# RMS norm sums in four 32-column strips behind the first early panel, with the gain folded into the operand split

## What is computed

```python
def rmsnorm(x, w):
    xf = x.astype(jnp.float32)
    y = xf * lax.rsqrt(jnp.mean(xf * xf, axis=-1, keepdims=True) + EPS)
    return (y * w.astype(jnp.float32)).astype(x.dtype)

def swiglu(h, w_gate, w_up, w_down):
    return (jax.nn.silu(h @ w_gate) * (h @ w_up)) @ w_down
...
    for layer in range(DEPTH):
        x = x + 0.5 * swiglu(rmsnorm(x, norm_ffn1[layer]), ffn1_gate[layer], ffn1_up[layer],
                             ffn1_down[layer])
        x = x + hybrid_mixer(rmsnorm(x, norm_mix[layer]), lb_all[layer], w_in[layer], hg_norm_w[layer],
...
        x = x + 0.5 * swiglu(rmsnorm(x, norm_ffn2[layer]), ffn2_gate[layer], ffn2_up[layer],
                             ffn2_down[layer])
    return rmsnorm(x, norm_final)
```

## Time and profile before

| | before |
|---|---|
| median of 3 runs | 1942.34 us |
| the profiled execution, its own time | 1941.35 us |
| its span in the trace | 1939.5 us |
| PE busy | 1803.8 us (93%) |
| PEld busy | 1736.4 us (90%) |
| DVE busy | 1086.5 us (56%) |
| ACT busy | 917.3 us (47%) |
| granted TensorE clock, mean | 0.971 |

### The profile page before, as it was taken

How to read it: one execution, slowest core, us unless ns; L and a number is a source line. 1 busy time by engine, 2 the same in 40 slices (tenths; PEclk the granted TensorE clock), 3 DMA queues, 4 the chain that set the end, 5 groups by cost and what they waited for, 6 DMA issues and landing times.

```text
span 1939.5 us, 34227 instructions
## 1 busy us (share of the span) xinstructions
PE 1803.8 (93%) x15120; PEld 1736.4 (90%) x15120; DVE 1086.5 (56%) x1231; ACT 917.3 (47%) x966; POOL 169.6 (9%) x120
## 2 busy tenths in 40 slices
PE   7999998899999999989889999999999888889997
PEld 7999897789999999988779999879897778889986
DVE  5544688464446544678555444644455555555555
ACT  5433675454335333566445344544444454534444
POOL 0000061000000000052000000683000000000000
PEclk9999998899999999998889999999999999999998
DMA  7555442135555555453035555456255414445541
GB/s 250 168 185 178 150 140 88 45 109 181 189 175 169 178 181 189 143 153 119 22 99 174 175 186 184 150 176 206 87 174 164 161 45 152 136 152 177 193 154 42
DMA packets 206531, 291.00 MB, mean 150 GB/s; under 512 B 4560, under 2 KB 170576, under 8 KB 206128
## 3 DMA queue, kind: packets, MB, share of 16 engines
q1 hardware_dynamic: 205936, 287.04, 45.4%
q0 software_dynamic: 448, 1.77, 0.3%
HBM read 287.75 MB, written 1.05 MB: 149 GB/s over the span
## 4 chain that ended last, share of the span: by engine, by line
PE 81%; DVE 11%; ACT 5%; issue 2%; DMA 0%; SPq 0%; ACTq 0%; DVEq 0%
PE colb L788 52%; PE acc L788 27%; DVE w_lo L1511 3%; PE aux L788 2%; ACT w_hi L1161 2%; DVE arena L1716 1%; DVE u L1571 1%; DVE x L1614 1%; DVE op_lo L1577 0%; DMA raw<-ffn_gate 0%; PE colb L1097 0%; ACT arena L1474 0%; DVE u L1629 0%; DVE x L1620 0%; DVE arena L1774 0%
## 5 line engine op out<-in xcount | busy, mean ns | idle before, releaser
L1511 DVE TENSOR_TENSOR w_lo<-raw,w_hi 128x2048 fp32r<-128x2048 f32 x271 | 622.1, 2296 | 625.6 <-ACT w_hi L1161 625.4
L1161 ACT ACTIVATE w_hi<-raw 128x2048 fp32r<-128x2048 f32 x271 | 515.7, 1904 | 430.5 <-PE acc L788 246.8
L788 PE MATMUL colb<-u_hi,w_hi 128*128 128x256 f32 x2256 | 644.2, 286 | 16.0 <-DVE w_lo L1511 15.9
L788 PE MATMUL colb<-u_lo,w_hi 128*128 128x256 f32 x2256 | 641.7, 284 | 0.0
L788 PE MATMUL colb<-u_hi,w_lo 128*128 128x256 f32 x2256 | 641.7, 284 | 0.0
L788 PEld LDWEIGHTS colb<-u_hi,w_hi 128*128 128x128 f32 x2256 | 436.5, 193 | 18.0 <-issue 11.9
L788 PEld LDWEIGHTS colb<-u_lo,w_hi 128*128 128x128 f32 x2256 | 436.7, 194 | 0.1
L788 PEld LDWEIGHTS colb<-u_hi,w_lo 128*128 128x128 f32 x2256 | 436.5, 193 | 0.0
L788 PE MATMUL acc<-op_hi,w_hi 128*128 128x256 f32 x1328 | 381.7, 287 | 22.5 <-DVE op_lo L1566 14.3
L788 PE MATMUL acc<-op_lo,w_hi 128*128 128x256 f32 x1328 | 379.5, 286 | 0.0
L788 PE MATMUL acc<-op_hi,w_lo 128*128 128x256 f32 x1328 | 379.1, 285 | 0.0
(11 more groups left out here) (298 smaller groups left out, 1784.1 us busy)
## 6 DMA issues: line engine op xcount, KB each, us to landing
raw<-w_in SPq DMA_DIRECT2D x78, 1024.0 KB, 5.1
raw<-ffn_gate SPq DMA_DIRECT2D x44, 1024.0 KB, 5.3
raw<-ffn_up SPq DMA_DIRECT2D x44, 1024.0 KB, 5.4
raw<-ffn_down SPq DMA_DIRECT2D x44, 1024.0 KB, 4.9
raw<-w_up SPq DMA_DIRECT2D x16, 1024.0 KB, 5.5
raw<-w_down SPq DMA_DIRECT2D x16, 1024.0 KB, 4.9
raw<-w_out SPq DMA_DIRECT2D x8, 1024.0 KB, 4.9
raw<-w_ret_out SPq DMA_DIRECT2D x8, 1024.0 KB, 4.9
```

The lines of the kernel that those rows point to most:

```text
L788: return pe.matmul(o, a, b, start=start, stop=stop, skip_group_check=True)
L1161: act.activation(split_view(w_hi, r), raw[:, p % RAW_SLOTS, 0:r["kt"] * r["nc"]], ACT.Copy)\
L1511: tt(split_view(w_lo, r), raw[:, p % RAW_SLOTS, 0:r["kt"] * r["nc"]], split_view(w_hi, r).bitcast(F32), ALU.subtract).then_inc(sem("w_lo_r ...
```

## The change

What it does, for each of the nine norms that feed a stage:

- On PE the norm sum no longer stands ahead of panel p. PE goes through panel p by chunks (`kk` outside, both halves `m` inside), and so through every column panel of kinds "A" and "B". Behind panel p come eight float32 matmuls with 32 columns of ones each, two for each of four strips of 32 output partitions (`parts`). ACT copies these partial sums to `rstd`, and in the middle of panel p+1 (`kk == 4`) one float32 matmul of the full ones matrix adds them (`parts_sum`, into the other half of `aux`). Since the strips hold 32 equal rows each, the scale of Ln is 1/(32 D).
- On ACT the rounding of `x * gain` reads `x` with the gain as the scale of the activation, two instructions of 128x256 for a chunk, with no wait for DVE. `w_hi` of p+1 stands between chunk 1 and chunk 2 instead of behind all; the squares of chunks 2 and 3 come last.
- On DVE `x_gained` is gone; the low part is one `scalar_tensor_tensor` of `x`, the gain and `op_hi` (two of 128x256 for a chunk), and `fill` makes `u32` from `x`, gain and `rstd` in the same way. `w_lo` of panel p is taken out of the panel before and stands behind the first chunk's update.

```diff
@@ -329,17 +329,17 @@
             early[1] = dict(n=count["fill"], panel=len(panels), ops=len(ops), **more)
             return count["fill"]
 
-        def norm_sum(src, next_="x_update"):
+        def norm_sum(src, next_="x_update", **more):
             count["norm"] += 1
-            step("norm_sum", n=count["norm"], src=src, x=count["x"], group=count["group"], next=next_, fill=count["fill"])
+            step("norm_sum", n=count["norm"], src=src, x=count["x"], group=count["group"], next=next_, fill=count["fill"], **more)
             return count["norm"]
 
         def pre_norm(gain, at):
 
 
             step("gained", gain=gain, at=at, n=count["fill"] + 1)
-            n = norm_sum("x", "fill")
-            f = fill(norm=n)
+            n = norm_sum("x", "fill", gain=gain, at=at)
+            f = fill(norm=n, gain=gain, at=at)
             return f
 
         def x_update(kind, **more):
@@ -828,26 +828,47 @@
                         if r["half"] == 1 and m == 0:
                             last.then_inc(sem("wide_first"), 1)
                 else:
-                    for m in range(max(r["nc"] // P, 1)):
-                        o = colb[:, r["c"] % 3, T * m:T * m + T]
-                        for kk in range(r["kt"]):
-                            xh, xl = r["xop"](kk)
-                            if m == 0 and kk % 2 == 0 and r.get("gained"):
-                                pe.wait_ge(sem("gained"), 4 * (r["gained"] - 1) + kk // 2 + 1)
-                            if m == 0 and kk % 2 == 0 and u_ready:
-                                pe.wait_ge(sem("u_ready"), u_ready - 3 + kk // 2)
+                    for kk in range(r["kt"]):
+                        xh, xl = r["xop"](kk)
+                        if kk % 2 == 0 and r.get("gained"):
+                            pe.wait_ge(sem("gained"), 4 * (r["gained"] - 1) + kk // 2 + 1)
+                        if kk % 2 == 0 and u_ready:
+                            pe.wait_ge(sem("u_ready"), u_ready - 3 + kk // 2)
+                        if kk == 4 and r.get("half") == 1:
+                            parts_sum(r)
+                        for m in range(max(r["nc"] // P, 1)):
+                            o = colb[:, r["c"] % 3, T * m:T * m + T]
                             m_ = slice(P * m, P * m + P)
...
                             for i, (a, b) in enumerate(trio):
-                                last = mm(o, a, b, kk == 0 and i == 0, kk == r["kt"] - 1 and i == 2)
+                                last = mm(o, a, b, kk == 0 and m == 0 and i == 0, kk == r["kt"] - 1 and i == 2)
+                    if r.get("gained"):
+                        last.then_inc(sem("panel_used"), 1)
+                        parts(r["norm"])
+                        return
                 last.then_inc(sem("panel_used"), 1)
 
+            def parts(n):
+
+                if n == 1:
+                    pe.wait_ge(sem("ones_set"), 1)
+                pe.wait_ge(sem("sq_ready"), 4 * n)
+                for kk in range(KD):
+                    g = slice(32 * (kk % 4), 32 * (kk % 4) + 32)
+                    last = mm(aux[g, 0:T], ones[:, 0:32], sq[:, kk, :], kk < 4, kk >= 4)
+                last.then_inc(sem("norm_parts"), 1)
+
+            def parts_sum(r):
+
+                pe.wait_ge(sem("parts_copied"), r["fill"]["n"])
+                mm(aux[:, T:2 * T], ones, rstd[:, :]).then_inc(sem("norm_summed"), 1)
+
             def norm_sum(r):
-                if r["n"] == 1:
-                    pe.wait_ge(sem("ones_set"), 1)
+                if r["next"] == "fill":
+                    return
                 for kk in range(KD):
                     if kk % 2 == 0:
                         pe.wait_ge(sem("sq_ready"), 4 * (r["n"] - 1) + kk // 2 + 1)
@@ -1239,13 +1260,26 @@
                 return act.activation(o, o, ACT.Exp, scale=-0.5, bias=b2)
 
             def norm_sum(r):
-                for b in range(4):
+                def chunk(b):
+                    if r["x"] == 0:
+                        act.wait_ge(sem(f"x_loaded{b}"), 16)
+                        act.wait_ge(sem("cols_loaded"), 16)
+                    else:
+                        act.wait_ge(sem("x_updated"), 4 * (r["x"] - 1) + b + 1)
+
+                def high(b):
+                    chunk(b)
+                    if b == 3:
+                        act.wait_ge(sem("panel_used"), r["panel"])
+                    for t in range(2):
+                        ins = act.activation(gained_chunk(op_hi, r["op"], b)[:, t, :], x[:, 2 * b + t, :], ACT.Copy,
+                                             scale=c(r["gain"], r["at"] + 2 * b + t))
+                    ins.then_inc(sem("g_hi_ready"), 1)
+
+                def square(b):
                     s = slice(2 * b, 2 * b + 2)
                     if r["src"] == "x":
-                        if r["x"] == 0:
-                            act.wait_ge(sem(f"x_loaded{b}"), 16)
-                        if r["x"]:
-                            act.wait_ge(sem("x_updated"), 4 * (r["x"] - 1) + b + 1)
+                        chunk(b)
                         src = x[:, s, :]
                     elif r["src"] == "acc":
                         bank_done(act, r, b)
@@ -1254,16 +1288,29 @@
                         act.wait_ge(sem("gated_ready"), b + 1)
                         src = gate_t[:, s, :]
                     act.activation(sq[:, s, :], src, ACT.Square).then_inc(sem("sq_ready"), 1)
-                    if r["src"] == "x" and r["next"] == "fill":
-                        act.wait_ge(sem("xg_ready"), 4 * r["fill"] + b + 1)
-                        if b == 3:
-                            act.wait_ge(sem("panel_used"), r["panel"])
-                        act.activation(gained_chunk(op_hi, r["op"], b), u32[:, s, :], ACT.Copy).then_inc(sem("g_hi_ready"), 1)
-                if r["next"] == "fill":
-                    split_hi_to(r["panel"] + (r["n"] > 1))
+
+                if r["next"] != "fill":
+                    for b in range(4):
+                        square(b)
+                    ln_exp_tables()
+                    act.wait_ge(sem("norm_summed"), r["n"])
+                    rstd_from(rstd[:, :], aux[:, 0:T], 1.0 / D).then_inc(sem("rstd_ready"), 1)
+                    return
+                for b in range(2):
+                    high(b)
+                    square(b)
+                if r["n"] > 1:
+                    split_hi_to(r["panel"] + 1)
+                for b in (2, 3):
+                    high(b)
+                for b in (2, 3):
+                    square(b)
+                split_hi_to(r["panel"] + 1)
+                act.wait_ge(sem("norm_parts"), r["fill"] + 1)
+                act.activation(rstd[:, :], aux[:, 0:T], ACT.Copy).then_inc(sem("parts_copied"), 1)
                 ln_exp_tables()
                 act.wait_ge(sem("norm_summed"), r["n"])
-                rstd_from(rstd[:, :], aux[:, 0:T], 1.0 / D).then_inc(sem("rstd_ready"), 1)
+                rstd_from(rstd[:, :], aux[:, T:2 * T], 1.0 / (32 * D)).then_inc(sem("rstd_ready"), 1)
 
...
@@ -1514,7 +1561,7 @@
             n_lo = [0]
 
             def split_lo_to(p):
-                while n_lo[0] <= min(p, n_panels - 1):
+                while n_lo[0] <= min(p, n_panels - 1) and not panels[n_lo[0]].get("gained"):
                     split_lo(panels[n_lo[0]])
                     n_lo[0] += 1
 
@@ -1565,16 +1612,13 @@
                 s = r["r"] % OP_SLOTS
                 tt(op_lo[:, s, :], src, op_hi[:, s, :].bitcast(F32), ALU.subtract).then_inc(sem("op_ready"), 1)
 
-            def x_gained(r, b):
-
-                for i in (2 * b, 2 * b + 1):
-                    ins = ts(u32[:, i, :], x[:, i, :], c(r["gain"], r["at"] + i), None, ALU.mult)
-                ins.then_inc(sem("xg_ready"), 1)
-
             def g_lo_(r, b):
                 dve.wait_ge(sem("g_hi_ready"), 4 * (r["n"] - 1) + b + 1)
-                s = slice(2 * b, 2 * b + 2)
-                tt(gained_chunk(op_lo, r["op"], b), u32[:, s, :], gained_chunk(op_hi, r["op"], b).bitcast(F32), ALU.subtract).then_inc(sem("gained"), 1)
+                hi, lo = gained_chunk(op_hi, r["op"], b), gained_chunk(op_lo, r["op"], b)
+                for t in range(2):
+                    ins = stt(lo[:, t, :], x[:, 2 * b + t, :], c(r["gain"], r["at"] + 2 * b + t), hi[:, t, :].bitcast(F32),
+                              ALU.mult, ALU.subtract)
+                ins.then_inc(sem("gained"), 1)
 
             def gained(r):
 
@@ -1583,12 +1627,12 @@
                         dve.wait_ge(sem(f"x_loaded{b}"), 16)
                     else:
                         update[0](b)
-                    x_gained(r, b)
+                    if b == (0 if r["nx"] else 3):
+                        split_lo(panels[n_lo[0]])
+                        n_lo[0] += 1
                     if b:
                         g_lo_(r, b - 1)
                 g_lo_(r, 3)
-                if r["nx"] == 0:
-                    split_lo_to(0)
 
             def fill(r, half):
 
```

(4 more changed lines are left out.)

## The result

The changed kernel takes 1998.97 us (median of 4 runs, 1998.74 to 1999.36); the kernel before took 1942.28 beside it. The ratio is 1.0271 (95%: 1.025 to 1.0291): slower by 57 us, 3 us more than forecast, inside the range. The profiled execution spans 1997.2 us, where the kernel before has 1939.5: 57.7 us more.

What follows compares the result with a forecast made beforehand. PE was taken as the bound, with the chain behind the norm sum delaying p+2. Later starts of p+2 (39.7 us) plus clock falls (14.4) gave 54.1, on 1941.35 and 1.0 for the median: 1996 us, range 1968 to 2009.

Steps and rivals of the forecast that it cites:

- What bounds the kernel: PE bounds it; a saving ahead of p+2 gives at most 1.3 us a boundary unless the `w_lo` chain starts earlier.
- T: Time origin at each boundary: start of the last `acc` matmul plus 0.12 us; 414.11 at the boundary worked through.
- The strips: Behind panel p: 16 strip records overlap to 56% and take 1.9 us; bounds 0.9 (four at a time) and 3.4 (serial).
- the rival: Strips run four at a time, 0.9 us instead of 1.9: 9 us less in all, 1987 us; chance 0.12.
- M: End of the full matmul that adds the strip sums in the middle of p+1; forecast 12.95 us behind the boundary's origin.
- From M to p+2: Chain Ln, Exp, `u32`, `u_hi`, `w_hi`, `w_lo` between the completed sum and p+2: 7.5 us with hand-overs.
- p+2: Its start moves from T+17.5 to T+20.45, +3.0 us at five like boundaries (210, 414, 610, 806, 1011 us).
- At 1213 and 1680: Later start of p+2 at these two boundaries: +5.35 us at 1213 and +7.4 us at 1680.
- The clock: Granted clock falls to 0.50 behind each new idle stretch ahead of p+2: 1.8 us at eight boundaries, 14.4 us.
- The loss stands in full: Everything later hangs on PE's panels, so no later wait absorbs the delay of p+2; the loss-given-back rival had chance 0.05.
- The other edits at nothing: Chunk order in ordinary panels, `x_gained` gone and extra ACT instructions were costed at nothing.
- The place of `w_lo` of p: Behind update 0 on DVE: a 2.21 us step that fits in at like boundaries, counted as delay at 1213 and 1680.

Runs made afterwards that it cites:

- experiment 10: Kernel before with the scalar-operand split, chunk order, and all four updates (DVE) and squares (ACT) first; full norm sum ahead of p: 1939.29 us, 0.9971.
- experiment 11: Kernel before with chunk order and all four updates and squares first, but its own operand split (`x_gained`) kept: 1937.76 us, 0.997.
- experiment 1: Changed kernel with `w_hi` of p+2 moved ahead of the table load and Ln, `w_lo` of p+2 ahead of `fill` half 0: 1961.69 us, 1.008.
- experiment 5: Changed kernel with the splits of p+2 moved early and `w_hi` of p+1 behind the rounding of chunks 2 and 3: 1953.5 us, 1.0047.
- experiment 8: Kernel before with strips alone: sum still ahead of p, two strips behind each chunk of squares, full matmul inside p: 1964.89 us, 1.0091.
- experiment 4: Changed kernel with 20 unused float32 matmuls filling PE's idle time ahead of p+2: 1985.54 us, 1.0203.
- experiment 2: Kernel before with the chunk order of column panels alone: 1946.15 us, 1.0003.
- experiment 7: Kernel before with the operand split alone: no `x_gained`, gain as scale on ACT, scalar operands on DVE: 1943.19 us, 0.9988.
- experiment 6: Changed kernel with `w_lo` of p put back in the panel before, ahead of the first update of x: 1995.73 us, 1.0263.
- experiment 3: Changed kernel with eight full matmuls behind panel p in place of strips, copy and the sum in p+1: 1975.36 us, 1.0147.

## Why the prediction was right, step by step

**What bounds the kernel** held. A saving on PE ahead of p+2 was said to be worth at most 1.3 us unless the chain to `w_lo` of p+2 starts earlier. Experiments 10 and 11 show this bound: PE is ready for p+2 at T+15.7 and 16.0, and p+2 starts 1.3 and 1.2 us earlier than in the kernel before, with Ln within 0.3 of where it was. They are the only ones clearly below the kernel before, by 0.3%. Experiments 1 and 5 take `w_lo` of p+2 out of the chain, and p+2 comes earlier than in the kernel before.

**The strips were mis-sized.** I took 1.9 us for 16 records, and argued from the two passes of a float32 matmul that they can't go four at a time. They take 1.07 with the last one's tail. In the trace four records start within 0.02 us, and the next four 0.22 to 0.24 later, about the step of one full record (0.215); in experiment 8, where only two strips are at hand, they start in pairs. So they do run four at a time. The Trainium skill (TensorE: Matmul & The Clock Gate, Part 3) says that packed tiles cost one matmul plus about 4 ns a tile. This trace agrees but for the size, 7 ns from start to start within a group. My row with alternating halves was not the nearest case. The change of shape costs something too: 0.21 us from the last colb start to the first strip, where a plain step is 0.12, and 0.31 from the last strip to the next colb, where the next group of strips comes 0.20 after a last strip. The Trainium skill, TensorEngine Tiling (Array Packing), Key Properties, says that a change of tiling mode drains the engine. The trace agrees in that there is a delay; it doesn't show the cause. The quicker strips brought only part of the 9 us that the rival gave them: M came at T+12.25 instead of 12.95, since panel p ended 0.2 later than worked out.

**From M to p+2** I had 7.5; it is 7.67. **p+2** came at T+19.95, forecast T+20.45: +2.46 instead of +3.0, five times. The wait of 1.2 us ahead of chunk 2, held by `w_hi` of p+1, stood where it was put. At the start p+2 came at 35.04 (forecast 35.75), at 1895 4.4 later than before (forecast 4.65).

**At 1213 and 1680 the terms were too small**, 6.6 for 5.35 and 8.1 for 7.4. M came as forecast at 1213 (T+22.5 against 22.3), but only because two errors cancel: p ended 1.1 us later than worked out, at the lower clock, and the strips took 0.9 less. Two things were missing. PE now stands idle for 6.1 us ahead of p (the first of these rows of its timeline) and for 5.7 ahead of p+2:

```profile
1249.08 0.55 PE L788 MATMUL colb<-op_hi,w_hi 128*128 128x256 f32 x1 [6.13 <-DVE op_lo L1619]
1270.36 0.55 PE L788 MATMUL colb<-u_hi,w_hi 128*128 128x256 f32 x1 [5.67 <-DVE w_lo L1558]
```

and the clock is 0.50 behind both (window, busy of PE, PEld, DVE, ACT, POOL, PEclk):

```profile
1249.08:1253.40 4.32, 4.32 (x20) 4.32 (x21) 3.54 (x10) 4.32 (x8) 1.64 (x3) 0.50 0.64 220
...
1270.36:1274.77 4.41, 4.41 (x21) 4.41 (x22) 3.93 (x8) 3.40 (x4) 4.08 (x5) 0.51 0.74 242
```

I had counted one fall a boundary. And the four `u` instructions took 2.49 us instead of 1.67 (below). This boundary and the way to the next cost 9.9 us for 7.15 forecast.

**The clock** was taken at 1.8 for eight boundaries, 14.4. Experiment 4 gives 13.4 us for all of it. That is right in the sum. It is not quite right in its parts: from one like boundary to the next filler gives 1.2 to 1.6 back (2.4 and 4.1 in the two stretches whose length varies by itself), and 1213 has two falls. At 414 us p+2 takes 7.7 us instead of 5.8, so the fall alone costs 1.9 there, near the 1.8 taken; filler gives only 1.2 of it back, because p+3 then waits for its `w_lo`.

**"The loss stands in full"** was right, and more: the whole is 57.7 us, of which 37.8 are p+2's later starts (39.7 forecast) and 19.9 what follows them. Filling the idle time gives 13.4 of these back (15.1 between the two profiled executions); the 0.7 at p+3 seen in experiment 4 makes 3.5 more at five boundaries. The remaining 1 to 3 us I have not placed. That the sum came within 3 us is in part luck: the five like boundaries were set 2.7 us too dear, those at 1213 and 1680 1.9 too cheap, and 5.5 us behind p+2 were in no term.

**The other edits at nothing**: right for the chunk order (experiment 2) and, within 0.1%, for the operand split (experiment 7). The place of `w_lo` of p had its own step in the prediction, which gave it a cost at 1213 and 1680 and none elsewhere. It costs 2 to 3 us there, but the move gains 1.15 at each like boundary, which the prediction did not see (experiment 6).

What the prediction had not seen is that its own number for a full sum in the strips' place would have been better: with 3.6 us behind p and no second step M is at about T+11, and experiment 3 gives 24 us back.

## What to carry to other kernels

Before work is taken off the busiest engine, follow the chain to the operands of the work behind it: here those hang on `rstd`. A saving on PE pays up to the slack of that chain (1.2 to 1.3 us at p+2 in experiments 10 and 11), and what makes `rstd` later than the slack allows costs, whatever PE saves. No run here made `rstd` come much earlier, so what that would bring isn't shown. A sum in two steps through another engine can be dear even if each step is short: in experiment 3 one slow step was 24 us better. And on PE a shorter piece between waits is not free: where it leaves PE idle for longer, the next panels may pay for it in clock, so look at the granted clock behind every place that gets lighter.
